# Summing mixture-of-experts rows in memory with weighted accumulating scatters, and fetching expert weights in halves, in a two-layer transformer trunk

## The chip, the cores and the metric

The kernel runs on one core of a Trainium2 chip. The metric is the device time of one execution in microseconds (us). The program is written engine by engine: TensorE (PE), VectorE (DVE), ScalarE (ACT), GpSimd (POOL) and SyncE (SP) each have their own instruction stream, and they meet only at semaphores.

## The reference, cut to what matters

Two layers, each an attention mixer followed by a mixture of experts; 1024 tokens of width 1024, all float32. The change touches the mixture of experts and the norm behind it:

```python
# hier_moe: top-1 group of 4, then top-2 of its 8 experts (32 experts, hidden width 512)
weights = g_gate * jax.nn.softmax(top_val, axis=-1)
h = jax.nn.silu(xb @ w_gate[e]) * (xb @ w_up[e])
out = h @ w_down[e]
y = jax.ops.segment_sum(out * row_w[:, None], row_tok, num_segments=n + 1)[:n]
# behind it, with DEEPNORM_ALPHA = 4 ** 0.25
x = layer_norm(DEEPNORM_ALPHA * x + y, gain, bias)
```

So each token has two (token, expert) pairs, 2048 in all, and the output of a token is the weighted sum of two expert rows.

## The kernel before

Each layer is two blocks of instructions. The first holds the start of the layer (for layer 1 the combine of layer 0: `Combine`) and the attention. The second, written by `Moe.run`, holds the mixer's output product with the first norm and the routing (`MixerOut`), and then the experts.

**Routing.** While TensorE computes the output product tile by tile (8 tiles of 128 tokens), VectorE norms each tile, and for groups of tiles (0 to 2, 3 to 5, 6, 7) it picks the experts (`choose`) and builds one-hot matrices (`select`, lines 1326 and 1327), from which TensorE lists in a PSUM bank which pair stands in which of 128 slots of each expert (`lists`). VectorE writes the list to `slot_rows`, with a column of token numbers and a column of pair numbers (lines 1360 to 1364, `slots_ready`). The two weights of a token (`w_pair`) are computed after that, from two exponentials of ScalarE (`exponentials`, `pair_weights`), token by token and not slot by slot. The normed rows go to `x_rows` in memory (L1078).

**Experts.** Loops over 32 experts, two to an iteration. For each expert POOL gathers its token rows by an indirect DMA (`gather`, L1618, two experts ahead), PE transposes them, and three weight matrices of 2 MB each (gate, up, down) come through one raw buffer each. To keep float32 accuracy each matrix and each input is split into a high and a low part: ScalarE makes the high part (L1769, in halves of 128x2048), VectorE the low one (L346), and PE does three passes (L1547 for gate and up, L1558 for down). SP refills a raw buffer as one DMA once both halves of its low part are made (`refill`, L1481). The result of an expert leaves PSUM by an ACT copy (L1799) and a DVE copy (L1867) into `res[b]`, b being the expert's parity. POOL then scatters it with an indirect DMA to `expert_rows`, one row per pair (`send`, `scatter`, L1624), and waits for it to land before it goes on to the next gather (`ahead`). `res_free` lets ACT and DVE write `res[b]` again once the scatter of two experts ago has landed. After expert 31 the same steps stand for extra blocks of an expert with over 128 rows (`extra_blocks`); none of them runs in the trace.

```python
pool.tensor_copy(row[b], column(e, 1)).then_inc(row_ready, 1)
pool.wait_ge(row_ready, 1 + e + 1)
pool.wait_ge(y_act, 1 + e + 1)
pool.wait_ge(y_dve, 1 + e + 1)
scatter(b, y_out[b])
pool.wait_ge(y_out[b], 16 * (i + 1))
pool.sem_inc(res_free, 1)
```

**Combine.** For each tile SP fetches three arrays of 128x1024: the first and second expert rows and the normed rows (`fetch_rows`, L1906 to L1908), four tiles ahead. The first four tiles are fetched at the end of the experts' block (`first_rows`), in layer 0 with three attention weight fetches behind them (`fetch_job`, L309). A new block starts on the engines once SP too has got to the end of the old one. Per tile ACT scales the first rows into PSUM (L1951), DVE adds the weighted second rows (L1959) and the ALPHA-scaled normed rows (L1963), takes mean and variance (L957 to L960), ACT applies the norm (L977), and POOL multiplies by the gain and adds the bias (L981, L985). In layer 0, PE transposes each tile, ACT and DVE split it, and the first projections of layer 1 start (L627). In layer 1 the tiles go to the output (L1938).

Of the kernel before, what the change touches and what calls it, by code (L numbers as in the profile page):

```python
# [8 lines left out]
F32 = mybir.dt.float32  # L9
# [7 lines left out]
P = 128  # L17
# [20 lines left out]
NO_ROW = 4 * PAIRS  # L38
# [154 lines left out]
def build(nc, x, ab_w_in, ab_w_out, ab_sinks, t5_bias, c_w_in, c_w_out, c_rel_bias, ln_gain, ln_bias,  # L193
          moe_w_group, moe_b_group, moe_w_router, moe_b_router, moe_w_gate, moe_w_up, moe_w_down, out):
    ctx = ExitStack()
    with ctx:
# [6 lines left out]
        o_dram = nc.dram_tensor("expert_rows", [PAIRS, D], F32).ap()  # L203
# [21 lines left out]
        w_pair = sb("w_pair", [P, 2, TILES])  # L225
        slot_rows = sb("slot_rows", [P, BLOCKS, 2], I32)
# [7 lines left out]
        pair_id = sb("pair_id", [P, ENTRIES])  # L234
# [120 lines left out]
        class Load:  # L355
# [3 lines left out]
            def __init__(self):  # L359
# [24 lines left out]
                def gpsimd(pool):  # L384
# [10 lines left out]
                    for group, f0 in zip(ROUTE_GROUPS, ENTRY):  # L395
                        for c in range(2):
                            f, n = f0 + c * len(group), len(group)
                            k.link(pool.iota(pair_id[:, f:f + n], pattern=[[2 * P, n]], base=2 * P * group[0] + c + 1,
                                             channel_multiplier=2, allow_small_or_imprecise_dtypes=True))
# [555 lines left out]
        def norm_begin(dve, rows, t, chain, var_ready):  # L955
# [4 lines left out]
            dve.tensor_scalar(st[:, 14:15], st[:, 13:14], LN_EPS, None, ALU.add).then_inc(var_ready, 1)  # L960
# [13 lines left out]
        def norm_apply(act, rows, t, scale_ready, normed):  # L974
            st = stats[:, t % 4, :]
            act.wait_ge(scale_ready, t + 1)
            act.activation(rows, rows, ACT.Identity, bias=st[:, 17:18], scale=st[:, 16:17]).then_inc(normed, 1)  # L977

        def norm_gain(eng, rows, gain, t, normed, gained):
            eng.wait_ge(normed, t + 1)  # L980
            eng.tensor_tensor(rows, rows, gain, ALU.mult).then_inc(gained, 1)  # L981
# [8 lines left out]
        class MixerOut:  # L990
# [4 lines left out]
            def __init__(self, layer, moe):  # L995
# [7 lines left out]
                 normed, x_turned, x_kept, x1_out, log_ready, log_kept, chain_sem, chosen_sent, rank_ready, ones_sent,  # L1003
                 list_done, slots_ready, exp_sent, exp_done, count_done, extra_sent, extra_done, extras_ready) = sems(
                     *[s + n for s in (
                         "x_in", "par_in", "gain_in", "yh_kept", "yl_kept", "wh_ready", "wl_ready", "mix_ready", "added",
                         "var_ready", "root_ready", "normed", "x_turned", "x_kept", "x1_out", "log_ready",
                         "log_kept", "chain", "chosen_sent", "rank_ready", "ones_sent", "list_done", "slots_ready",
                         "exp_sent", "exp_done", "count_done", "extra_sent", "extra_done", "extras_ready")])
                self.x1_out, self.slots_ready, self.extras_ready = x1_out, slots_ready, extras_ready  # L1010
# [3 lines left out]
                most = 2 * max(len(group) for group in ROUTE_GROUPS)  # L1014

# [1088 lines left out]
```

## Time and profile before

| what | us |
|---|---|
| median of 3 runs | 2539.83 |
| lowest, highest of them | 2538.68, 2542.66 |
| the profiled execution | 2548.89 |
| its span, first to last instruction | 2547.1 |
| PE busy in the span | 2285.8 |
| DVE busy | 1792.9 |
| ACT busy | 1400.6 |
| POOL busy | 514.1 |

The rows further down come from the profiled execution, so times in them are positions in a span of 2547.1 us; layer 0's experts run from about 570 to 1174 us, its combine to about 1262 us, layer 1's experts from about 1877 to 2483 us and its combine to the end. A row of the timeline has the start, the duration, engine, line, operation and operands; in brackets stands how long the engine had been idle before it and what it had waited for. Busy shares of PE are of little use alone; what counts is which wait ends last in each stretch.

### The profile page before, as it was taken

What the parts mean: (1) busy time and instruction counts of PE and PEld (TensorE: products, weight loads), DVE (VectorE), ACT (ScalarE), POOL (GpSimd) and SP (SyncE); (2) the same over time, 40 slices, a digit from 0 to 9 for tenths busy, and PEclk for the clock granted to TensorE, in tenths of its full rate; (3) what the DMA queues carried; (4) which work ended last, traced back from release to release, by engine and by line L of the source; (5) the groups of instructions that cost most, each with busy time, mean ns of one, the idle gap of its engine ahead of it and who ended that gap; (6) DMA issues with size and microseconds to landing.
All of it is one profiled execution on the core that took longest, in us unless ns stands there. A gap on an engine that the chain in (4) does not pass through costs nothing. (4 is left out here: it accounts for less than half of the span.)

```text
span 2547.1 us, 35618 instructions
## 1 busy us (share of the span) xinstructions
PE 2285.8 (90%) x12656; PEld 1860.6 (73%) x12656; DVE 1792.9 (70%) x2475; ACT 1400.6 (55%) x1689; POOL 514.1 (20%) x434
## 2 busy tenths in 40 slices
PE   7999997969999999993699999989969999999980
PEld 6767776857888787882577778867757878887770
DVE  4565546568898889894645555555678988898875
ACT  3454445027877777772344444443057777877743
POOL 0002333012232233321500000000012222332215
PEclk9999998979999999996799999999979999999995
DMA  4110113238999999985411111104069999999956
GB/s 126 24 35 18 34 34 103 91 143 320 371 367 365 371 373 374 369 349 183 169 44 37 44 36 36 36 34 177 34 258 362 381 378 381 378 364 352 361 204 264
DMA packets 127444, 533.53 MB, mean 209 GB/s; under 512 B 36161, under 2 KB 76121, under 8 KB 102761
## 3 DMA queue, kind: packets, MB, share of 16 engines
q1 hardware_dynamic: 108560, 498.44, 52.3%
q0 software_dynamic: 18432, 33.60, 3.5%
q8 instruction: 66, 1.08, 0.2%
q14 instruction: 42, 0.34, 0.0%
q10 hardware_dynamic: 344, 0.08, 0.0%
HBM read 515.21 MB, written 50.39 MB: 222 GB/s over the span
## 5 line engine op out<-in xcount | busy, mean ns | idle before, releaser
L346 DVE TENSOR_TENSOR arena<-arena,arena 128x2048 fp32r<-128x2048 f32 (+1 forms) x458 | 956.5, 2123 | 94.8 <-ACT arena L1769 76.4
L1769 ACT CAST arena<-arena 128x2048 fp32r<-128x2048 f32 x384 | 712.4, 1917 | 140.5 <-PE psum L1547 98.2
L1547 PE MATMUL psum<-arena,arena 128*128 128x512 f32 x3072 | 736.5, 395 | 8.6 <-DVE arena L346 8.6
L1547 PEld LDWEIGHTS psum<-arena,arena 128*128 128x128 f32 x3072 | 570.8, 189 | 124.9 <-issue 6.2
L627 PE MATMUL psum<-arena,arena 128*128 128x512 f32 x2016 | 508.7, 403 | 4.0 <-DVE arena L346 3.1
L627 PEld LDWEIGHTS psum<-arena,arena 128*128 128x128 f32 x2016 | 371.8, 190 | 98.0 <-issue 12.0
L1558 PE MATMUL psum<-arena,arena 128*128 128x512 f32 x1536 | 368.7, 396 | 10.6 <-DVE arena L346 10.6
L1558 PEld LDWEIGHTS psum<-arena,arena 128*128 128x128 f32 x1536 | 288.7, 190 | 85.5 <-DVE arena L346 25.2
L337 PE MATMUL psum<-ident,arena 128*128 128x128 f32 x1024 | 156.9, 295 | 111.9 <-POOL arena L985 39.0
L346 DVE TENSOR_TENSOR arena<-psum,arena 128x512 fp32r<-128x512 f32 (+1 forms) x186 | 161.0, 873 | 130.8 <-ACT arena L1788 64.4
L337 PEld LDWEIGHTS psum<-ident,arena 128*128 128x128 f32 x1024 | 144.8, 197 | 138.9 <-POOL arena L985 42.7
L765 ACT ACTIVATE arena<-arena,arena 128x640 f32<-128x640 f32 (+4 forms) x192 | 120.0, 626 | 193.4 <-DVE arena L847 147.8
L1125 PE MATMUL psum<-arena,arena 128*128 128x512 f32 x768 | 185.3, 397 | 9.3 <-ACT arena L342 6.3
L717 ACT COPY arena<-psum 128x512 f32<-128x512 f32 (+3 forms) x288 | 120.2, 467 | 131.6 <-PE psum L658 131.4
L1615 POOL COPY arena<-slot_rows 128x1 int32 (+1 forms) x64 | 58.1, 907 | 646.8 <-DMA expert_rows<-arena,arena 576.7
L1125 PEld LDWEIGHTS psum<-arena,arena 128*128 128x128 f32 x768 | 142.8, 189 | 39.6 <-issue 6.8
L658 PE MATMUL psum<-ident,arena 128*128 128x128 f32 x888 | 134.5, 283 | 22.2 <-POOL arena L951 9.3
L1618 POOL DMA_INDIRECT arena<-x_rows,arena x64 | 138.0, 2157 | 55.0 <-POOL arena L1615 49.6
L658 PEld LDWEIGHTS psum<-ident,arena 128*128 128x128 f32 x888 | 109.0, 144 | 51.8 <-POOL arena L951 12.1
L680 PE MATMUL psum<-arena,arena 128*64 128x128 f32 x1776 | 131.3, 290 | 0.0
L847 DVE CUSTOM_DVE_ANT_0 arena<-psum,arena 128x640 f32<-128x640 f32 (+3 forms) x192 | 104.9, 572 | 33.6 <-PE psum L646 33.2
L646 PE MATMUL psum<-arena,arena 64*128 64x320 f32 (+5 forms) x1056 | 116.8, 341 | 10.7 <-DVE arena L847 9.5
(155 smaller groups left out, 1783.1 us busy)
## 6 DMA issues: line engine op xcount, KB each, us to landing
arena<-in_moe_w_gate SPq DMA_DIRECT2D x64, 2048.0 KB, 10.8
arena<-in_moe_w_up SPq DMA_DIRECT2D x64, 2048.0 KB
arena<-in_moe_w_down SPq DMA_DIRECT2D x64, 2048.0 KB, 8.9
arena<-expert_rows SPq DMA_DIRECT2D x32, 512.0 KB, 6.7
x_rows<-arena SPq DMA_DIRECT2D x24, 512.0 KB, 2.6
arena<-x_rows SPq DMA_DIRECT2D x24, 512.0 KB, 8.0
arena<-in_c_w_in SPq DMA_DIRECT2D x24, 512.0 KB, 4.1
arena<-in_x SPq DMA_DIRECT2D x16, 512.0 KB, 7.1
```

The source lines that it names most:

```text
L337: m = pe.transpose(dst_bank[:, j * P:(j + 1) * P], rows[:, c0 + j:rows.shape[1]:stride], ident[:])
L346: return eng.tensor_tensor(tile, src, high.bitcast(F32), ALU.subtract)
L627: mm = pe.matmul(job_bank(i, g), w[:, c * P:(c + 1) * P], xs[:, c, half_cols(g)], start=(a == 0), stop=(a == 23))
L658: mm = pe.transpose(bank(B_TURN + h)[:, (b - 4 * g) * P:(b - 4 * g + 1) * P], probs_of(s, h)[:, b * P:(b + 1) * P], ident[:])
L680: mm = pe.matmul(bank(B_OUT)[DH * h:DH * (h + 1), (t % 4) * P:(t % 4 + 1) * P], v_r[pair.kv][:, (kt + b) * P + DH * h:(kt + b) * P + DH * ...
L717: copy(probs_t[s % 2][h][:, a:b], bank(B_TURN + h)[:, 0:b - a]).then_inc(t_copied[h], 1)
L765: act.activation(probs_a[s % 2][h][:, 0:ahead + nk], biased[h][:, 0:ahead + nk], ACT.Exp, bias=low[s % 2][h], scale=-1.0, accum_out=rowsum ...
L1125: return pe.matmul(bank(2 * (t % 2) + half), ys[:, c, t * P:(t + 1) * P], w[:, c, half * BANK:(half + 1) * BANK], start=(k == 0 and c == 0 ...
L1547: mm = pe.matmul(bank(o), cs[:, c * P:(c + 1) * P], ws[:, c * FF:(c + 1) * FF], start=(k == 0 and c == 0), stop=(k == 2 and c == CH - 1))
L1558: mm = pe.matmul(bank(B_Y + s), hs[:, c * P:(c + 1) * P], ws[:, c * D + s * BANK:c * D + (s + 1) * BANK], start=(k == 0 and c == 0), stop= ...
L1618: pool.indirect_dma_start(out=rows[b], out_offset=None, in_=x1_dram, in_offset=bass.IndirectOffsetOnAxis(ap=token[b], axis=0), bounds_chec ...
L1769: act.copy(w_hi[w][:, cols], self.raw[w][:, cols]).then_inc(hi_ready[w], 1)
```

## The change

- `expert_rows` with a row per pair goes; a new array `summed_rows` (`h_dram`) has one row per token. SP writes each normed tile into it, beside the write to `x_rows`. The scatter of each expert adds into it (`compute_op=ALU.add`), at the token's number. Where `slot_rows` had two columns it has one.
- The weights are computed earlier, in three parts for tiles 0 to 2, 3 to 5, and 6 and 7, and are listed slot by slot with the pairs: `lists` multiplies 64 columns instead of 32 for the first two parts, and four more products (`list_weights`) do the last. VectorE keeps them in `slot_weights`.
- For each expert POOL also copies the slot weights to `row_weight[b]`. The two copies out of PSUM become multiplications by it, and wait for it (`weight_ready`).
- A weight fetch of 2 MB becomes two of 1 MB, each with a semaphore of its own: SP refills a half as soon as its low part is made, and ACT starts on a half as soon as it has landed.
- The combine fetches one array per tile. ALPHA goes into the norm's variance and gain; no addition is left. The gain is multiplied by DVE (from PSUM), no longer by POOL. Only two tiles are fetched ahead of the block's end, and the attention weight fetches stand in the next block.

The diff, cut to what this text speaks of (`...` marks what is left out):

```diff
@@MixerOut.sync
                         sp.dma_start(x1_dram[t * P:(t + 1) * P, :], rows_all[:, t, :]).then_inc(x1_out, 16)
+                        sp.dma_start(h_dram[t * P:(t + 1) * P, :], rows_all[:, t, :]).then_inc(h_out, 16)
@@MixerOut.tensor
+                def list_weights(pe):
+                    pe.wait_ge(weights_sent, 1)
+                    for a in range(ENTRIES - late):
+                        mm = pe.matmul(bank(B_LIST)[:, E:2 * E], at_slot[:, a, :], at_block[:, a, E:2 * E],
+                                       start=False, stop=(a == ENTRIES - late - 1), skip_group_check=True)
+                    mm.then_inc(weights_listed, 1)
@@MixerOut.vector
+                def make_weights(dve, L, k):
...
+                    dve.wait_ge(exp_done, k + 1)
+                    L(dve.tensor_reduce(gate[:, ts], gexp[:, ts, :], AX.X, ALU.add))
+                    L(dve.tensor_scalar(near[:, ts], gap[:, ts], 1.0, ALPHA, ALU.add, ALU.mult))
+                    L(dve.tensor_tensor(near[:, ts], near[:, ts], gate[:, ts], ALU.mult))
+                    L(dve.reciprocal(w0, near[:, ts]))
+                    L(dve.tensor_tensor(w1, w0, gap[:, ts], ALU.mult))
...
+                            if g < 2:
+                                dve.tensor_scalar(at_block[:, a, E:2 * E], down_cols[:], key[:, f:f + 1],
+                                                  weight[:, f:f + 1], ALU.is_equal, ALU.mult)
...
                     norm(7)
+                    make_weights(dve, L, 1)
                     select(1)
                     choose(2)
                     keep_logits(7)
                     choose(3)
+                    send_gaps(2)
                     select(2)
                     select(3)
...
-                    L(dve.tensor_copy(slot_rows[:, 0:E, 1], listed))
-                    dve.tensor_scalar(slot_rows[:, 0:E, 0], slot_rows[:, 0:E, 1], 1, None, ALU.arith_shift_right
-                                      ).then_inc(slots_ready, 1)
+                    dve.tensor_copy(slot_rows[:, 0:E], listed).then_inc(slots_ready, 1)
@@Moe.run, SP
-                        sp.wait_ge(lo_ready[w], 1 + 2 * e)
-                        settle(sp)
-                        self.fetch(sp, e, w)
+                        for s in range(2):
+                            sp.wait_ge(lo_ready[w], 1 + 2 * (e - 1) + s + 1)
+                            settle(sp)
+                            self.fetch_half(sp, e, w, s)
@@Moe.run, POOL
-                        pool.indirect_dma_start(out=o_dram, out_offset=bass.IndirectOffsetOnAxis(ap=row[b], axis=0),
+                        pool.indirect_dma_start(out=h_dram, out_offset=bass.IndirectOffsetOnAxis(ap=row[b], axis=0),
                                                 in_=res[b], in_offset=None,
-                                                bounds_check=PAIRS - 1, oob_is_err=False).then_inc(sem, 16)
+                                                bounds_check=SEQ - 1, oob_is_err=False,
+                                                compute_op=ALU.add).then_inc(sem, 16)
...
                     ahead(2, 1, 0)
+                    pool.wait_ge(before.weights_kept, 1)
+                    pool.wait_ge(before.h_out, 16 * TILES)
...
-                        pool.tensor_copy(row[b], column(e, 1)).then_inc(row_ready, 1)
+                        pool.tensor_copy(row_weight[b], column(slot_weights, e)).then_inc(weight_ready, 1)
+                        pool.tensor_copy(row[b], column(slot_rows, e)).then_inc(row_ready, 1)
@@Moe.run, ACT
-                        act.wait_ge(self.raw_in[w], 1 + 16 * (e + 1))
                         act.wait_ge(used[w], 1 + e)
                         for s in range(2):
+                            act.wait_ge(self.raw_in[w][s], 1 + 16 * (e + 1))
...
+                        act.wait_ge(weight_ready, 1 + e + 1)
+                        act.mul(res[b][:, 0:BANK], bank(B_Y), row_weight[b]).then_inc(y_act, 1)
@@Moe.run, DVE
                     split(GATE, 0)
+                    before.send_weights(dve)
                     split(UP, 0)
-                    before.pair_weights(dve)
+                    before.keep_weights(dve)
...
+                        dve.wait_ge(weight_ready, 1 + e + 1)
+                        dve.tensor_scalar(res[b][:, BANK:2 * BANK], bank(B_Y + 1), row_weight[b], None, ALU.mult
+                                          ).then_inc(y_dve, 1)
@@Combine
             def first_rows(self, sp):
-                for t in range(4):
+                for t in range(2):
                     self.fetch_rows(sp, t)
-                if not self.last:
-                    for i in range(3):
-                        fetch_job(sp, 1, i)
...
+                    for t in range(2, TILES):
+                        self.rows_here(sp, t - 2)
+                        self.fetch_rows(sp, t)
+                        if 3 <= t < 6 and not last:
+                            fetch_job(sp, 1, t - 3)
                     for t in range(TILES):
-                        if t + 4 < TILES:
-                            sp.wait_ge(summed, t + 1)
-                            self.fetch_rows(sp, t + 4)
                         sp.wait_ge(shifted, t + 1)
...
                     for t in range(TILES):
-                        norm_gain(pool, rows[t], ln_pars[:, 0, :], t, normed, gained)
                         norm_shift(pool, rows[t], ln_pars[:, 1, :], t, gained, shifted)
...
                     for t in range(TILES):
-                        add(dve, t)
-                        if t >= 1:
-                            norm_scale(dve, t - 1, chain, root_ready, scale_ready)
-                        moments(dve, chain, t)
+                        norm_scale(dve, t, chain, root_ready, scale_ready)
+                        if t + 1 < TILES:
+                            moments(t + 1)
+                        gain(t)
```

How the instructions stand on two engines, before and now. First POOL, one half of an iteration of the experts' loop; DMA on L1618 and L1686 is the gather, on L1624 and L1692 the scatter, `ISA` and `REGISTER_ALU` are register work. Before:

```order
L1615 COPY arena_5574<-slot_rows 128x1
L1616 REGISTER_ALU
L1618 DMA arena_5562<-x_rows,arena_5574 128x1024
L1649 ISA
L1649 COPY arena_5575<-slot_rows 128x1
L1650 REGISTER_ALU
L1624 DMA expert_rows<-arena_5567,arena_5575 2048x1024
```

And now:

```order
L1683 COPY arena_5570<-slot_rows 128x1
L1684 REGISTER_ALU
L1686 DMA arena_5558<-x_rows,arena_5570 128x1024
L1720 ISA
L1720 COPY arena_5573<-slot_weights 128x1
L1721 REGISTER_ALU
L1721 COPY arena_5571<-slot_rows 128x1
L1722 REGISTER_ALU
L1692 DMA summed_rows<-arena_5563,arena_5571 1024x1024
```

One copy, that of the weights, stands between the gather and the copy of the rows; the scatter keeps its place.

Then SP at the end of layer 0's experts, up to the block's end (`UNCONDITIONAL_BRANCH` of L2071, now L2135) and a little beyond; `arena` tiles are on-chip buffers. Before, from the last of the first four tiles:

```order
L1906 DMA arena_5506<-expert_rows 128x1024
L1907 DMA arena_5510<-expert_rows 128x1024
L1908 DMA arena_5514<-x_rows 128x1024
L309 DMA arena_54<-in_c_w_in 128x8x128
L309 DMA arena_55<-in_c_w_in 128x8x128
L309 DMA arena_56<-in_c_w_in 128x8x128
L2071 UNCONDITIONAL_BRANCH
```

And now:

```order
L1984 DMA arena_5506<-summed_rows 128x1024
L1984 DMA arena_5507<-summed_rows 128x1024
L2135 UNCONDITIONAL_BRANCH
L587 UNCONDITIONAL_BRANCH
L1984 DMA arena_5508<-summed_rows 128x1024
L1984 DMA arena_5509<-summed_rows 128x1024
L310 DMA arena_54<-in_c_w_in 128x8x128
```

Fifteen DMAs stood ahead of the block's end; two do now, and the attention weights come behind it.

## Rows read from the trace of the kernel before

**Rows 1.** Stretches: core 0, PE, PEld, DVE, ACT, POOL busy (count), PE clock, DMA, GB/s

```profile
618.20:1132.90 514.70, 505.62 (x2356) 414.73 (x2354) 459.09 (x281) 399.91 (x296) 149.93 (x110) 1.00 0.96 371
1174.40:1262.50 88.10, 29.72 (x137) 24.93 (x137) 51.33 (x86) 32.50 (x46) 40.35 (x16) 0.61 0.62 219
2483.50:2547.10 63.60, 0.00 (x0) 0.00 (x0) 34.73 (x64) 21.16 (x25) 37.38 (x16) 0.50 0.69 264
```

**Rows 2.** Timeline, from layer 0's last scatter to layer 1's first projection

```profile
1169.72 0.98 POOL L1624 DMA_INDIRECT expert_rows<-arena,arena  x1 [12.25 <-DVE arena L1867]
...
1183.09 12.62 SPq L309 DMA_DIRECT2D arena<-in_c_w_in  x3
1196.39 2.15 ACT L1951 ACTIVATE psum<-arena,w_pair 128x1024 f32<-128x1024 f32 x2 [27.73 <-PEq L2071]
...
1240.62 6.68 PE L627 MATMUL psum<-arena,arena 128*128 128x512 f32 x24
```

**Rows 3.** The DMA issues of the page: KB each, median us to landing

```profile
arena<-in_c_w_in SPq DMA_DIRECT2D x24, 512.0 KB, 4.1
```

**Rows 4.** Timeline, DVE in the two combines: layer 0, then layer 1

```profile
1233.56 1.28 DVE L1959 SCALAR_TENSOR_TENSOR psum<-arena,w_pair,psum 128x1024 f32<-128x1024 f32 x1
1234.87 1.22 DVE L1963 SCALAR_TENSOR_TENSOR arena<-arena,psum 128x1024 f32<-128x1024 f32 x1
...
1241.14 1.28 DVE L1959 SCALAR_TENSOR_TENSOR psum<-arena,w_pair,psum 128x1024 f32<-128x1024 f32 x1
...
2503.07 1.28 DVE L1959 SCALAR_TENSOR_TENSOR psum<-arena,w_pair,psum 128x1024 f32<-128x1024 f32 x1
...
2507.47 1.28 DVE L1959 SCALAR_TENSOR_TENSOR psum<-arena,w_pair,psum 128x1024 f32<-128x1024 f32 x1
```

**Rows 5.** The chain that ended last, layer 1's end: start, us, what

```profile
2479.32 3.21 DMA expert_rows<-arena,arena
...
2487.64 10.79 DMA arena<-x_rows
...
2541.69 2.38 POOLq L2071
```

**Rows 6.** Timeline, POOL, one round of the experts' loop in layer 1

```profile
2204.15 1.02 POOL L1624 DMA_INDIRECT expert_rows<-arena,arena  x1 [1.53 <-DVE arena L1867]
2214.37 1.45 POOL L1615 COPY arena<-slot_rows 128x1 int32 x1 [9.20 <-DMA expert_rows<-arena,arena]
2216.67 2.66 POOL L1618 DMA_INDIRECT arena<-x_rows,arena  x1 [0.85 <-POOL arena L1615]
2219.33 1.33 POOL L1649 COPY arena<-slot_rows 128x1 int32 x1
2222.20 1.02 POOL L1624 DMA_INDIRECT expert_rows<-arena,arena  x1 [1.53 <-DVE arena L1867]
```

**Rows 7.** Waits of POOL, 600 to 1140 us: total, times, longest

```profile
POOL arena L1615 <- DMA expert_rows<-arena,arena: 289.2, 28, 13.1
```

**Rows 8.** Timeline, POOL, after a scatter late in layer 0's experts

```profile
1138.26 0.18 POOL L1649 COPY arena<-slot_rows 128x1 int32<-128x1 int32 x1 [2.41 <-DMA expert_rows<-arena,arena]
```

**Rows 9.** The DMA queues of the page: packets, MB, share of 16 engines

```profile
q1 hardware_dynamic: 108560, 498.44, 52.3%
q0 software_dynamic: 18432, 33.60, 3.5%
```

**Rows 10.** Timeline, DVE in layer 0's routing and at the experts' start

```profile
504.95 0.20 DVE L1248 TENSOR_TENSOR logits<-psum,b_route 128x36 f32<-128x36 f32 x1 [2.52 <-PE psum L1097]
...
545.19 0.28 DVE L1326 TENSOR_SCALAR arena<-iota_cols,arena 128x128 f32<-128x128 f32 x1
545.39 0.30 DVE L1327 TENSOR_SCALAR arena<-down_cols,arena,pair_id 128x32 f32<-128x32 f32 x1
...
567.60 0.18 DVE L1375 TENSOR_REDUCE arena<-arena 128x8 f32<-128x32 f32 x1
...
568.96 1.22 DVE L346 TENSOR_TENSOR arena<-psum,arena 128x1024 fp32r<-128x1024 f32 x1
```

**Rows 11.** The chain that ended last, layer 1's second expert: start, us, what

```profile
1939.93 11.43 DMA arena<-in_moe_w_up
```

More of the change, by code:

```diff
@@ L952, in _, with norm_begin @@
                                                left[h][:, SEQ - nk:SEQ], ALU.subtract).then_inc(p_ready[h], 1)
-        def norm_begin(dve, rows, t, chain, var_ready):
+        def norm_begin(dve, rows, t, chain, var_ready, factor=1.0):
             st = stats[:, t % 4, :]
@@ L972, in norm_scale, with norm_apply, norm_gain @@
                               ).then_inc(scale_ready, 1)
-        def norm_apply(act, rows, t, scale_ready, normed):
+        def norm_apply(act, out, rows, t, scale_ready, normed):
             st = stats[:, t % 4, :]
             act.wait_ge(scale_ready, t + 1)
[L977 to L981, printed above, removed]
+            act.activation(out, rows, ACT.Identity, bias=st[:, 17:18], scale=st[:, 16:17]).then_inc(normed, 1)
+        def norm_gain(dve, rows, src, factor, gain, t, normed, gained):
+            dve.wait_ge(normed, t + 1)
+            dve.scalar_tensor_tensor(out=rows, in0=src, scalar=factor, in1=gain, op0=ALU.mult, op1=ALU.mult
+                                     ).then_inc(gained, 1)
         def norm_shift(pool, rows, shift, t, gained, shifted):
@@ L1032, in __init__ @@
                 rank = place(AT_CHOICE + 1, ENTRIES)
+                weight = place(AT_CHOICE + 1.0625, ENTRIES)
                 count_row = place(AT_CHOICE + 1.25, E)
@@ L1309, in choose, with send_gaps @@
                             L(ins)
+                    def send_gaps(k):
+                        ts = WEIGHT_TILES[k]
+                        nt = ts.stop - ts.start
+                        L(dve.tensor_tensor(gexp[:, ts, :], logits[:, ts, 0:G],
+                                            gmax[:, ts].unsqueeze(2).to_broadcast([P, nt, G]), ALU.subtract))
+                        dve.tensor_tensor(gap[:, ts], m2[:, ts], m1[:, ts], ALU.subtract).then_inc(exp_sent, 1)
                     def select(g):
@@ L1511, in run @@
                 row = [pen(8)[:, 0:1].bitcast(I32) for _ in range(2)]
+                row_weight = [pen(8)[:, 0:1] for _ in range(2)]
                 assert pen.kb <= AT_GATE - 12
@@ L1703, in _ @@
                     pe.wait_ge(rows_ready, 1 + 1)
+                    before.list_weights(pe)
                     turn(0, 0, 0)
@@ L1772, in _ @@
                     split(GATE, 0)
+                    before.exponentials(act, 2)
                     split(UP, 0)
-                    before.exponentials(act)
                     act.wait_ge(before.x1_out, 16 * TILES)
+                    act.wait_ge(before.h_out, 16 * TILES)
                     act.wait_ge(xt_ready, 1 + 1)
```

200 lines of the change are left out of this document (106 added, 94 removed).

## The prediction

> **What bounds the kernel now.** I first cut the span into stretches. In the experts' loop [rows 1] TensorE is busy 505.6 of 514.7 us at its full clock of 2.4 GHz, and the DMA engines are busy 0.96 of the time: two resources near their limit together. 28 experts take 514.7 us, 18.38 us each. The two combines are another matter. Layer 0's takes 88.1 us with PE busy for 29.7 of them at a mean clock of 0.61; layer 1's takes 63.6 us with no PE work at all. Neither is bound by work: DVE, the busiest, has 51.3 and 34.7 us.
>
> Then the timeline across layer 0's combine [rows 2]. The last scatter is issued at 1169.72. ACT starts its first scaling at 1196.39, 26.7 us later, released at the block's end, which SP reached only when it had got rid of three weight fetches that took it 12.62 us from 1183.09 on. The twelve row fetches ahead of them fill the queue. In layer 1 the chain that ended last [rows 5] goes from the last scatter (landed at 2482.5) through row fetches (a piece of 10.79 us) and then down POOL's gain and bias to the end.
>
> **The change, term by term**, on the profiled execution's span of 2547.1 us.
>
> *Layer 0's combine.* SP now has two fetches before the block's end. I let the last scatter land 1 us later than now (below), which puts the first fetch at 1175.4; a fetch of 512 KB lands after about 4.1 us [rows 3], on empty queues 3.5 (I choose the lower), so DVE begins near 1179. Its work per tile falls from 7.58 us (1233.56 to 1241.14 [rows 4]) by the two additions of 1.28 and 1.22, and rises by one multiplication out of PSUM like L1959, 1.28: 6.36 us where splits of tiles and weights lie between, and 4.40 - 1.22 = 3.18 without them. Moments and first root take 2.5 us; tiles 0 to 2 at 3.2, tile 3 at 4.6, tiles 4 and 5 at 6.4, and a part of tile 6 until tile 3's low part is made (4.6) give 1179 + 2.5 + 9.6 + 4.6 + 12.8 + 4.6 = 1213. There PE starts the first projection, now at 1240.62 [rows 2]: 27 us earlier. From there to the stretch's end at 1262.5 it is PE and its transposes as before. I take **-26**.
>
> *Layer 1's combine.* First fetch at 2484.5, rows at 2488, scale at 2490.5, seven tiles at 3.2, a last one at 3.1, the bias on POOL 2.4 and the store 3.1 (the end now comes 5.4 us after 2541.69 [rows 5], of which POOL has 2.38): 2521.5. I take **-25**; POOL, with one pass per tile in place of two, is no longer the pace; DVE's 3.2 is, and ACT's one pass per tile fits beside it.
>
> *Routing.* From tile 7's norm to the list DVE is late and has next to no idle time. A small operation costs 0.20 there (545.19 to 545.39 [rows 10]); chained ones 0.22 (six between 567.60 and 568.96). Added ahead of `slots_ready`: five chained for the weights of part 1 (1.1), six one-hots (1.2), `send_gaps` (0.4); one conversion goes (-0.2): +2.5. Behind it: weights of part 2 and four one-hots (1.9) and a copy (0.2), against the 1.36 of `pair_weights` and the 0.4 of the old exponent inputs: +0.3, and I add 0.5 for PE's four products in front of the first transposes. **+3.3 per layer, +6.6**. The same additions for part 0 lie in a gap of 2.52 in which DVE waits for the router's logits [rows 10], against 2.2 added, and cost nothing; if that cover went, it would be 2.2. The table changes of ACT for its early exponentials lie in its long waits for DVE's variances. The eight more writes of rows are issued while the queue has little else; only tile 7's stands in front of the first up weights (about 1.3 us at the rate of the page), and half fetches give that back.
>
> *The experts' loop, ACT and DVE.* One pass out of PSUM stays one pass. Two more semaphore waits lie on the ACT path that delays the second expert of an iteration; at 0.05 to 0.1 each, **+4** over 32 iterations (ends: 0 and 8). In layer 1 ACT twice waited for up weights, once with a landing of 11.43 [rows 11], at about 1 us lost each; a half arrives sooner: **-1.6**.
>
> *The experts' loop, POOL.* This is the place that can go wrong. Before, nobody but POOL waited for the ring scatter, landing, gather, copy; ACT and DVE only needed a scatter two experts back. Now both stop in front of `weight_ready`, and behind them stand the next SiLU and both next splits. The ring [rows 6]: scatter 1.02, landing 9.20, token copy 1.45, 0.85, gather 2.66, copy 1.33, and then only 1.53 us, most of it handover, until the next scatter: 18.05 in all. With the weight copy in the row copy's place, evacuations (0.7, an estimate: half of the 1.28 of a pass twice as wide [rows 4]) and handover (1.0 of the 1.53) behind it, the new ring is 9.0 plus the landing, or 8.6 with a shorter token copy; it sets the pace once landings exceed about 9.6. They now average 289.2 / 28 = 10.3 in the stretch [rows 7], so they must become shorter. Uncontended, the landing takes 2.41 [rows 8]: some 7 us are the weight traffic. One 2 MB fetch occupies the engines for 52.3% x 2547.1 x 2.10 / 498.44 = 5.6 us [rows 9], so this is a little over one fetch. With fetches of half the size I expect the 7 us to become about 4. The accumulation is in no row. Below, it costs nothing more than the plain scatter; above, each row is read and written, one after the other, as if the scatter came twice, 2.41 us. I take 1.3, since only the reading is new (the software queue's 3.5% is 0.7 us a transfer, on half the engines if valid rows stand in the first slots 1.4). Landing: 2.4 + 4 + 1.3 = 7.7, two below the limit. **0**.
>
> The Trainium skill, page "DMA: Bandwidth & Descriptors", section "Queues, rings and completion order", says that each DMA engine goes round its queues and changes only at the end of a packet of several descriptors. By that the scatter waits for at most the packet in progress, which a half fetch halves, and the term would be the same 0; the landings agree that the waiting is about one fetch. The skill's page "Collectives: The Full Stack", section "Part 3: Why 7× under link rate — side-by-side accounting", speaks against the change: an addition in a DMA needs two reads per piece, so it delivers half as fast. No row here shows an accumulation; by that rule the landing would still be under the limit.
>
> Sum: 2547.1 - 26 - 25 + 6.6 + 4 - 1.6 = 2505, which is 42 less. The profiled execution took 2548.89, 9 us over the median of 2539.83, so the median becomes **2498**.
>
> **Rivals.**
>
> *A, POOL sets the pace (slower).* If halves don't shorten the landing and the addition costs 1.4, it is 11.7 and the ring 20.3: 1.9 us over 18.4, for 62 experts 118 us, 2616. It decides from 0.65 us per expert on (40 / 62), a landing of about 10.3. For it: the landings of 13.1 and a ring that is already full. Against: 2.41 alone, which says the length is that of the traffic. 14%.
>
> *B, the DMA engines become the bound.* Per expert, three fetches of 5.6 and two indirect transfers of 0.7 make 18.2 of 18.38 us [rows 9]; a further 0.7 for the reading makes 18.9, 0.5 too much for 62 experts: 31 us, 2529. For it: the 0.96 [rows 1]. Against: packets stretched by each other are in these shares, and halves refill earlier. 12%.
>
> *C, the combines are paced by fetches.* Only two are in flight; at 8 us to landing instead of 4 that is 4 us a tile and not 3.2, and with exchanges between DVE and ACT no better than now each gains some 8 us less: 2514. 12%.
>
> *D, it is a wash*: several of these partly, 2535 to 2545. 2%.
>
> **How the numbers follow.** The forecast has 60%. A measurement of this kernel can tell 0.2%, 5 us, from no change. All of the forecast, B and C and none of A lie below 2534.8: faster 0.84, same 0.02, slower 0.14. The range leaves out A: it starts 14 us under the forecast (loop terms at their low ends, combines 5 us better each) and goes up to 2535, over B.
>
> **What would show it.** The span from the last scatter of layer 0 to the first projection falls from 71 to 44 us; ACT or DVE starts the combine within 8 us of the scatter's landing; the last 63.6 us become about 38. DVE sets 3.2 us per tile in layer 1. The experts' period stays 18.3 to 18.5 us, the median landing of the scatter is 6 to 9 us, and POOL waits for DVE before it scatters. Wrong it would be if the evacuations waited for POOL's weight copy and PE showed idle time before gate or down products at a period over 18.7; B would show as ACT waiting for weights.

## The result and the profile after

The changed kernel takes **2559.74 us** (median of 5 runs, 2554.12 to 2569.66) against 2539.83 of before (2538.68 to 2554.17, 5 runs): a ratio of 1.0068 with a 95% interval of 1.0043 to 1.0092, slower by 0.7%. The prediction was 2498, faster by 1.6%. The profiled execution took 2569.66 us, with a span of 2567.9 against 2547.1 before: 20.8 more.

I cut both spans at five places that a timeline names: the first gate product (PE's first product with an expert's gate weights) and the last scatter of each layer, and the end. The last column has the terms of my sum.

| stretch | before | after | difference | my terms |
|---|---|---|---|---|
| start to first gate product, layer 0 | 570.33 | 589.10 | +18.8 | +3.3 |
| experts, layer 0, to the last scatter | 599.4 | 618.5 | +19.1 | +2 |
| last scatter to first gate product, layer 1 | 706.9 | 699.2 | -7.7 | -26 + 3.3 |
| experts, layer 1, to the last scatter | 602.7 | 616.0 | +13.3 | +0.4 |
| last scatter to the end | 67.8 | 45.1 | -22.7 | -25 |

**The combines** did what the change says. Layer 0's last scatter, SP's first fetches, DVE's first moments and PE's first projection, in the timeline after (columns: start us, us, engine, line, operation, tiles, idle time before and its releaser), where [rows 2] stood:

```profile
1207.58 1.57 POOL L1692 DMA_INDIRECT summed_rows<-arena,arena  x1 [12.07 <-issue]
...
1214.85 6.36 SPq L1984 DMA_DIRECT2D arena<-summed_rows  x4
...
1220.55 0.69 DVE L959 BATCH_NORM_STATS2 stats<-arena 128x6 f32<-128x512 f32 x1 [10.69 <-PEq L2135]
...
1224.49 1.21 DVE L983 SCALAR_TENSOR_TENSOR arena<-psum,arena 128x1024 f32<-128x1024 f32 x1
...
1227.56 1.22 DVE L983 SCALAR_TENSOR_TENSOR arena<-psum,arena 128x1024 f32<-128x1024 f32 x1
...
1254.73 6.99 PE L628 MATMUL psum<-arena,arena 128*128 128x512 f32 x24
```

From scatter to projection it is 47.2 us, before 70.9. DVE begins 13 us after the scatter; before, the first instruction, ACT's, came 26.7 us after it. Without splits DVE makes a tile in 3.07 us (1224.49 to 1227.56). Layer 1's combine does the same, 22.7 us less.

**The experts' loop** got slower. A pair of experts (one iteration) takes 38.06 us in the median, before 36.76. The waits between 700 and 1150 us, of the kernel before and then of the change (us in total, times, longest):

```profile
POOL arena L1615 <- DMA expert_rows<-arena,arena: 240.7, 23, 13.1
...
PE psum L337 <- DVE arena L1852: 5.3, 12, 0.4
```

```profile
POOL arena L1683 <- DMA summed_rows<-arena,arena: 196.6, 24, 9.0
...
ACT arena L1876 <- POOL arena L1720: 31.6, 11, 2.9
...
PE psum L338 <- DVE arena L1931: 19.8, 12, 1.8
```

The landing (the time until a scatter's rows are in memory) did become shorter. But ACT's evacuation (L1876) waited for POOL's weight copy (L1720) in 11 of the 24 experts there, once per iteration, and PE waits at the transposes of the hidden rows (L338) for DVE's product of gate and up (L1931) 12 times, once per iteration, 1.2 us longer each (19.8 less 5.3, by 12). The timeline of one iteration shows why it is every second expert; PE's two down products are L1625:

```profile
943.88 1.61 POOL L1692 DMA_INDIRECT summed_rows<-arena,arena  x1 [1.83 <-DVE arena L1947]
...
952.53 0.75 PE L338 MATMUL psum<-ident,arena 128*128 128x128 f32 x4 [1.74 <-DVE arena L1931]
...
955.33 5.74 PE L1625 MATMUL psum<-arena,arena 128*128 128x512 f32 x24 [0.20 <-DVE arena L347]
...
958.41 1.31 POOL L1720 COPY arena<-slot_weights 128x1 f32 x1
...
961.11 0.69 ACT L1876 ACTIVATE arena<-psum,arena 128x512 f32<-128x512 f32 x1 [2.15 <-PE psum L1625]
...
963.52 1.61 POOL L1692 DMA_INDIRECT summed_rows<-arena,arena  x1 [1.59 <-DVE arena L1947]
...
972.96 2.21 POOL L1683 COPY arena<-slot_rows 128x1 int32 x1 [7.83 <-DMA summed_rows<-arena,arena]
...
973.22 5.62 PE L1625 MATMUL psum<-arena,arena 128*128 128x512 f32 x24
...
976.02 2.64 POOL L1686 DMA_INDIRECT arena<-x_rows,arena  x1 [0.85 <-POOL arena L1683]
...
978.66 1.31 POOL L1720 COPY arena<-slot_weights 128x1 f32 x1
...
980.09 0.69 ACT L1876 ACTIVATE arena<-psum,arena 128x512 f32<-128x512 f32 x1 [2.87 <-POOL arena L1720]
```

The two experts of an iteration are not alike. From a scatter to the end of the next down product it is 943.88 to 961.07, 17.2 us, on one side and 963.52 to 978.84, 15.3 us, on the other. POOL's scatter, landing, token copy, gather and weight copy take 15.8 and 16.5 us. On the first side the weight is 1.4 us early; on the second it is 1.1 us late, and both evacuations with it. Behind ACT's stand the next SiLU, the copies of the next tokens and two splits, and behind these DVE's product, for which PE then waits 1.74 us (0.4 before).

**The experts' start** takes longer in both layers, in three pieces. The first is in the mixer's product. ACT's instructions from the norm's root of tile 3 to that of tile 4, before and then after:

```profile
482.58 0.20 ACT L965 ACTIVATE stats<-stats 128x1 f32<-128x1 f32 x1 [9.30 <-DVE stats L960]
486.38 1.02 ACT L1198 COPY arena<-psum 128x1024 f32<-128x1024 f32 x1 [3.60 <-PE psum L337]
496.68 0.20 ACT L965 ACTIVATE stats<-stats 128x1 f32<-128x1 f32 x1 [9.28 <-DVE stats L960]
```

```profile
485.85 0.20 ACT L967 ACTIVATE stats<-stats 128x1 f32<-128x1 f32 x1 [9.28 <-DVE stats L962]
486.07 1.28 ACT L1240 ACT_TABLE_LOAD   x1
494.42 0.21 ACT L1240 ACTIVATE arena<-arena 128x12 f32<-128x12 f32 x1 [7.07 <-DVE arena L1361]
...
494.64 0.99 ACT L1220 COPY arena<-psum 128x1024 f32<-128x1024 f32 x1
...
506.73 0.20 ACT L967 ACTIVATE stats<-stats 128x1 f32<-128x1 f32 x1 [9.80 <-DVE stats L962]
```

The copy of the turned rows (L1198, now L1220) used to come 3.8 us after the root. Now the early exponentials stand ahead of it, and wait until DVE has finished choosing the experts of the first three tiles (part 0). The copy comes 8.8 us after the root, PE waits for it with the router's product, and the next root comes 20.9 us after the last instead of 14.1: **+6.8**. The other two pieces lie behind it. From tile 7's root to POOL's first token copy it is 21.1 instead of 18.8 us, **+2.3**. From that copy to the first transposes it is 13.5 instead of 7.0, **+6.5**:

```profile
558.72 0.20 POOL L1615 COPY arena<-slot_rows 128x1 int32<-128x1 int32 x1 [19.93 <-DVE slot_rows L1364]
558.79 8.89 DVE L346 TENSOR_TENSOR arena<-arena,arena 128x2048 fp32r<-128x2048 f32 x4
...
559.92 2.27 POOL L1618 DMA_INDIRECT arena<-x_rows,arena  x1 [0.99 <-POOL arena L1615]
...
563.31 0.33 SPq L1481 DMA_DIRECT2D arena<-in_moe_w_gate  x1
...
565.68 1.95 PE L337 MATMUL psum<-ident,arena 128*128 128x128 f32 x8 [8.06 <-DMA arena<-x_rows,arena]
```

```profile
570.85 4.49 DVE L347 TENSOR_TENSOR arena<-arena,arena 128x2048 fp32r<-128x2048 f32 x2
571.07 2.12 POOL L1683 COPY arena<-slot_rows 128x1 int32<-128x1 int32 x1 [22.22 <-DVE slot_rows L1424]
574.19 2.26 POOL L1686 DMA_INDIRECT arena<-x_rows,arena  x1 [1.00 <-POOL arena L1683]
...
575.37 0.80 SPq L1543 DMA_DIRECT2D arena<-in_moe_w_gate  x2
...
584.60 1.97 PE L338 MATMUL psum<-ident,arena 128*128 128x128 f32 x8 [5.40 <-DMA arena<-x_rows,arena]
```

Before, two small operations of DVE (the old inputs of the exponentials) stood between the list and the first weight split, and POOL's copy slipped in ahead of the split by 0.07 us. Now the split follows the list at once, and the copy takes as long as the split's first half. The gather leaves when SP is already issuing the gate fetch that the same split released, and lands 10.4 us after its issue began, not 5.8.

So per layer 15.6 us at the start, 32.4 us in both loops, -23.8 and -22.7 us in the combines: +17.1. Most of the remaining 3.7 us lie in layer 0 ahead of all that: the first norm root already comes 1.7 us later, and the roots of tiles 1 and 2 are 11.4 us apart and not 9.8, with a granted clock of 0.93 in 450 to 500 us where it was 1.00 (in e4, which leaves this part as it was, they are 11.4 apart too). In the profiles of this study the first root lies between 444.7 and 452.7 us, which is why I judge every experiment by its stretches and not by its median alone.

### The profile page after: what moved, and what is told of

It is laid out like the page before. It is cut to its first block and busy times, and to the rows that moved or that the text cites. A ratio compares the mean times of both kernels' runs of the same rounds, so it can differ in the third digit from the quotient of the medians.

```text
span 2567.9 us, 36470 instructions
## 1 busy us (share of the span) xinstructions
PE 2305.8 (90%) x12672; PEld 1877.3 (73%) x12672; DVE 1788.5 (70%) x2519; ACT 1400.7 (55%) x1689; POOL 646.6 (25%) x482
## 5 line engine op out<-in xcount | busy, mean ns | idle before, releaser
L628 PEld LDWEIGHTS psum<-arena,arena 128*128 128x128 f32 x2016 | 372.9, 191 | 97.7 <-issue 11.6
L1625 PE MATMUL psum<-arena,arena 128*128 128x512 f32 x1536 | 369.7, 397 | 8.6 <-DVE arena L347 8.6
L1625 PEld LDWEIGHTS psum<-arena,arena 128*128 128x128 f32 x1536 | 290.9, 191 | 82.1 <-DVE arena L347 20.9
L338 PE MATMUL psum<-ident,arena 128*128 128x128 f32 x1024 | 157.5, 296 | 112.9 <-DVE arena L1931 50.4
L338 PEld LDWEIGHTS psum<-ident,arena 128*128 128x128 f32 x1024 | 145.5, 198 | 140.3 <-DVE arena L1931 64.4
L1683 POOL COPY arena<-slot_rows 128x1 int32 (+1 forms) x64 | 69.9, 1092 | 532.9 <-DMA summed_rows<-arena,arena 459.9
L1686 POOL DMA_INDIRECT arena<-x_rows,arena x64 | 174.7, 2729 | 55.0 <-POOL arena L1683 55.0
L1692 POOL DMA_INDIRECT summed_rows<-arena,arena x64 | 102.9, 1607 | 187.5 <-DVE arena L1947 175.5
L1876 ACT ACTIVATE arena<-psum,arena 128x512 f32<-128x512 f32 x64 | 44.0, 688 | 173.5 <-PE psum L1625 106.9
```

Of the source, the lines that this page charges most:

```text
L338: m = pe.transpose(dst_bank[:, j * P:(j + 1) * P], rows[:, c0 + j:rows.shape[1]:stride], ident[:])
L628: mm = pe.matmul(job_bank(i, g), w[:, c * P:(c + 1) * P], xs[:, c, half_cols(g)], start=(a == 0), stop=(a == 23))
L1625: mm = pe.matmul(bank(B_Y + s), hs[:, c * P:(c + 1) * P], ws[:, c * D + s * BANK:c * D + (s + 1) * BANK], start=(k == 0 and c == 0), stop= ...
L1686: pool.indirect_dma_start(out=rows[b], out_offset=None, in_=x1_dram, in_offset=bass.IndirectOffsetOnAxis(ap=token[b], axis=0), bounds_chec ...
```

## Experiments

**My theory** was then: three separate losses, (a) the weight copy at the end of POOL's ring, (b) the early exponentials in front of a copy, (c) the token copy beside the split. The rivals: the DMA engines set the pace because of the addition (rival B), the halves cost more than they bring, or the second set of row writes delays the start.

| run | median us | ratio to before (95%) | experts, layers 0, 1 | median pair | last scatter to end |
|---|---|---|---|---|---|
| change | 2559.74 | 1.0068 (1.0043 to 1.0092) | 618.5, 616.0 | 38.06 | 45.1 |
| e1 weights early | 2534.26 | 0.9952 (0.9935 to 0.9969) | 602.2, 602.0 | 36.84 | 45.3 |
| e2 plain scatter | 2522.78 | 0.9912 (0.9889 to 0.9936) | 600.2, 601.3 | 36.84 | 42.1 |
| e3 whole fetches | 2598.91 | 1.0211 (1.0178 to 1.0244) | 639.9, 635.7 | 39.66 | 45.1 |
| e4 before, halves | 2543.27 | 1.0000 (0.9984 to 1.0017) | 600.4, 600.1 | 36.75 | 68.2 |
| e5 exponentials later | 2551.68 | 1.0033 (1.0017 to 1.0049) | 616.5, 617.1 | 38.06 | 45.5 |
| e6 weights before split | 2549.87 | 1.0022 (1.0008 to 1.0036) | 616.0, 617.6 | 38.05 | 45.5 |
| e7 e1 + e5 + e6 | 2506.09 | 0.9867 (0.9838 to 0.9895) | 602.7, 601.6 | 36.87 | 45.4 |
| e8 tokens early | 2529.53 | 0.9953 (0.9939 to 0.9968) | 602.2, 602.0 | 36.87 | 45.6 |
| e9 weight last | 2585.77 | 1.0156 (1.0128 to 1.0183) | 626.5, 626.3 | 38.58 | 45.4 |
| e10 all early | 2502.82 | 0.9845 (0.9829 to 0.9861) | 602.2, 601.6 | 36.86 | 45.3 |

**e1: the weight copy ahead of the landing.**

```diff
+                    def weigh(e, b):
+                        pool.tensor_copy(row_weight[b], column(slot_weights, e)).then_inc(weight_ready, 1)
+
+                    weigh(0, 0)
+
                     def send(e, i, b):
...
-                        pool.tensor_copy(row_weight[b], column(slot_weights, e)).then_inc(weight_ready, 1)
                         pool.tensor_copy(row[b], column(slot_rows, e)).then_inc(row_ready, 1)
...
                         scatter(b, y_out[b])
+                        if not isinstance(e, int) or e < EXPERTS - 1:
+                            weigh(e + 1, 1 - b)
...
                         pool.wait_ge(y_out[b], 16 * (i + 1))
```

> The changed kernel, with GpSimd copying the next expert's weight column right behind its scatter and no longer behind the landing, token copy and gather. Theory (the weight copy at the end of GpSimd's ring delays the evacuations of every second expert by about 1.2 us, and TensorE's hidden transposes with them): ACT and DVE no longer wait for the weight copy, a pair of experts takes 36.7 to 37.0 us instead of 38.06, the time falls by 30 to 38 us, to 2522 to 2530. Rival (the DMA engines set the pace, because of the addition's reads or the halves): waits move to the weights, a pair stays above 37.6 us, and the time stays at 2550 to 2560.

The pair is at 36.84 and 30 us of the loops are gone (16.3 and 14.0). The median fell by 25.5, less than the 30 to 38 that I had given, and lies above my 2522 to 2530. By the ratios it is 29 us: the kernel before, measured again beside each group of runs, had medians from 2539.8 to 2542.3. No evacuation waits for POOL. The scatter lands no sooner than in the change (10.1 us from issue, there 9.5), and the DMA engines are busier than there (0.98 of the time against 0.96), so neither of these was the bound. But their waits did appear, as rival B said (waits of e1, 700 to 1150 us), and they cost a little that the median pair does not show: both loops take 1204.2 us here and 1201.5 in e2.

```profile
ACT arena L1850 <- DMA arena<-in_moe_w_gate: 28.0, 22, 2.3
...
PE psum L338 <- DVE arena L1937: 6.8, 12, 0.6
```

**e2: a scatter that overwrites** (`compute_op=ALU.add` taken away; the sums are left out).

> The changed kernel with a scatter that overwrites in place of one that adds (the sums over a token's two experts and its own row are left out). Theory: the addition costs 0.6 us at the issue and about 2 us of landing, so the landing falls from 9.4 to 7 to 8 us from the issue, the weight copy comes early enough, and the loop runs at about 36.9 us a pair; each combine begins 2.5 us earlier. Together 35 to 42 us less, 2518 to 2526. Rival (the landing is all weight traffic, the addition costs nothing beyond its issue): pairs at 37.5 to 38 us, 2545 to 2560. Rival (reads of the addition load the DMA engines): also a fall, but with DMA's share visibly lower and waits for weights gone.

The landing falls from 9.5 to 7.7 us, the pair to 36.84, the last stretch by 3.0 us. The addition thus costs 1.8 us from issue to landing in the loop, 0.6 of it at the issue itself, and 3.0 us at the end. The DMA issues of 700 to 1150 us (median us to landing), of the change, of this run and of e4:

```profile
summed_rows<-arena,arena POOLq DMA_INDIRECT x23, 9.5
```

```profile
summed_rows<-arena,arena POOLq DMA_INDIRECT x25, 7.7
```

```profile
expert_rows<-arena,arena POOLq DMA_INDIRECT x24, 7.8
```

**e3: whole fetches in the change** (one transfer of 2 MB a matrix, released by the second low part, as before).

> The changed kernel with each weight matrix fetched by one transfer of 2 MB again. Theory: the scatter lands 1.5 to 3 us later, GpSimd's ring of 9.0 us plus the landing then exceeds 18.4 us for every expert, and the loop takes 20 to 21 us an expert: 2600 to 2680. Rival (two issues and two semaphores a matrix cost more than they bring): the time falls, to 2540 or lower.

A hair under its low end: 39 us over the change, 19.8 an expert and not 20 to 21. ACT now waits for the weight copy (here L1719) in 22 of 23 experts:

```profile
ACT arena L1876 <- POOL arena L1719: 77.6, 22, 5.0
```

From copy to first transposes it is still 13.1 us: the halves are not what delays the start.

**e4: halves in the kernel before.**

> The kernel before with weight fetches in halves, nothing else. Theory (halves only shorten what waits in the queues, and nothing there waits for them but the few up weights of layer 1): within 5 us of the kernel before, 2533 to 2542, the scatter's landing 1 to 3 us shorter than the 10.3 us wait of before. Rival (halves burden SyncE and the DMA engines): slower than before by 10 to 30 us.

No change in time: the ratio is 1.0000, and the median lies 1 us above the 2533 to 2542 that I had given. The landing falls by 3.6 us, from 11.4 to 7.8. POOL alone waits for it, and nobody waits for POOL. From copy to first transposes it is 7.0 and 6.9 us.

**e5: the exponentials behind the copy.**

```diff
-                        if t == 7:
-                            exponentials(act, 1)
+                        if t in (4, 7):
+                            exponentials(act, t // 7)
                         norm_root(act, t, var_ready, root_ready)
-                        if t == 3:
-                            exponentials(act, 0)
```

> The changed kernel with ACT's exponentials of the first three tiles behind its copy of tile 3's turned rows, no longer ahead of it. Theory (ACT stands in front of the exponentials until DVE has finished the whole choice of part 0, and the router's product of tile 3 and every later tile wait behind it): the interval between the norm roots of tiles 3 and 4 falls from 20.9 to 14.1 us in both layers, 13 us less, 2544 to 2550. Rival (the 6.8 us are the two table loads or the added writes of rows): the interval stays over 19 us and the time at 2555 to 2562.

The roots of tiles 3 and 4 stand 14.1 us apart again in both layers, and the table load behind the copy is still there, in a wait of 9 us:

```profile
477.43 0.20 ACT L967 ACTIVATE stats<-stats 128x1 f32<-128x1 f32 x1 [9.28 <-DVE stats L962]
481.24 1.02 ACT L1220 COPY arena<-psum 128x1024 f32<-128x1024 f32 x1 [3.60 <-PE psum L338]
482.27 1.28 ACT L1238 ACT_TABLE_LOAD   x1
...
491.54 0.20 ACT L967 ACTIVATE stats<-stats 128x1 f32<-128x1 f32 x1 [3.90 <-DVE stats L962]
```

The median fell by 8.1 us where the two intervals give 13.6; it lies 2 us above what I expected. The interval of its ratio touches the change's, so it is the stretch that shows this gain and not the median.

**e6: the last weights ahead of the first split** (`before.send_weights(dve)` moved up in front of `split(GATE, 0)`).

> The changed kernel with DVE making the last tiles' weights and one-hots ahead of the first weight split, no longer behind it. Theory (GpSimd's copy of the token column took 2.12 us beside the split instead of 0.2, the gather then left together with the gate fetch that the split releases, and landed 5 us later): from the copy to the first transposes 7 to 8 us instead of 13.5, in both layers; 10 to 13 us less, 2547 to 2551. Rival (the gather is slow because of the weight halves or the second set of row writes in the queues): 12 to 13.5 us as now, no gain.

From copy to first transposes it is now 5.5 us in both layers, 8 us less. But the next token copy met the splits:

```profile
570.13 0.19 POOL L1683 COPY arena<-slot_rows 128x1 int32<-128x1 int32 x1 [22.24 <-DVE slot_rows L1424]
...
571.32 1.24 POOL L1686 DMA_INDIRECT arena<-x_rows,arena  x1 [1.00 <-POOL arena L1683]
571.79 8.88 DVE L347 TENSOR_TENSOR arena<-arena,arena 128x2048 fp32r<-128x2048 f32 x4
...
572.58 8.14 POOL L1683 COPY arena<-slot_rows 128x1 int32<-128x1 int32 x1
...
575.66 1.97 PE L338 MATMUL psum<-ident,arena 128*128 128x128 f32 x8 [1.76 <-DMA arena<-x_rows,arena]
...
582.05 1.19 PE L1614 MATMUL psum<-arena,arena 128*128 128x512 f32 x2 [4.42 <-DVE arena L347]
```

DVE's low part of the first rows now comes behind four splits, so the first gate product follows the copy by 11.9 us (18.0 in the change, 11.6 before): 6.1 us gained there. The median fell by 9.9, the low end of what I had given.

**e7: all three.**

> The changed kernel with all three: weight columns copied ahead of the landing, exponentials behind the copy, last weights ahead of the split. Theory: the three losses are separate stretches and add up, 25 + 13 + 12 us under the changed kernel: 2505 to 2514. Rival (they overlap, or one delay hides behind another): 2518 to 2530.

2506.09: 53.6 us under the change and 1.3% under the kernel before. By the ratios to before, the three singly took away 1.2%, 0.4% and 0.5% (of 0.7% slower), together 2.0%; e7 took away 2.0%. The losses add up, and the rival of overlapping losses is out.

**e8: only the token copy ahead of the landing**, the weight copy left where it was (the column for expert e + 4 is copied behind scatter e; the gather stays).

> The changed kernel with only the token column of the gather after next copied ahead of the landing; the weight copy stays behind landing and gather. Theory (what counts is when GpSimd's weight copy ends against the end of the down product, whichever piece of the ring is taken out): the weight comes 1.4 to 3 us earlier, no evacuation waits for it, a pair takes 36.8 to 36.9 us, 2530 to 2540. Rival (the evacuations suffer from the weight copy itself standing beside them, not from its being late): a pair stays at 38 us, 2555 to 2560.

36.87 us a pair, and 2529.53, half a microsecond under the range that I had given. It is not the weight copy as such that costs; it is when it ends.

**e9: the two copies in the other order**, rows first, weight second.

> The changed kernel with GpSimd's two copies in the other order, the scatter's rows first and the weights second. Theory: the row copy takes 0.2 us on one side of a pair and up to 2.2 on the other, where DVE is in a split, and both now stand ahead of the evacuations: a pair takes 38.3 to 40 us, 2565 to 2620. Rival (no dependence on the copy's time): 2555 to 2562.

38.58 us a pair, and 8 and 10 us more than the change in the two loops. Both sides are late now (waits of e9, 700 to 1150 us):

```profile
ACT arena L1876 <- POOL arena L1721: 71.4, 23, 3.2
```

**e10: the three, and every copy of POOL ahead of the landing**, both first token columns ahead of the first gather.

> The three fixes, and in addition token and row columns copied ahead of the landing, and at the start of the experts both token columns copied ahead of the first gather (the second one took 8.14 us beside the splits with the three fixes). Theory: the loop is at TensorE's pace already, so only the start gains, 0 to 4 us a layer: 2499 to 2506. Rival (something of GpSimd's ring still shows in the loop): a pair falls under 36.7 us and the time under 2498.

2502.82, the fastest, 1.5% under the kernel before; the interval overlaps with e7's, so the two can't be told apart. The pair does not fall: POOL no longer sets anything in the loop. At the start the second gather's own issue takes 8.65 us beside the splits in place of the copy, and nothing is gained there.

## Why the prediction was wrong

**The ring, "it sets the pace once landings exceed about 9.6": this is the step that failed.** I held POOL's ring against the mean period of 18.4 us, but the weight copy must be in time on each side of a pair. From a scatter to the end of the next down product it is 15.4 us on one side and 16.2 on the other already in the kernel before (medians from 700 to 1150 us), 15.3 and 16.3 in e1 and e2. By my own terms [rows 6] scatter, token copy, handover, gather and weight copy take 1.02 + 1.45 + 0.85 + 2.66 + 1.33 = 7.3 us beside the landing, which leaves 8.0 on the short side. I had the landing at 7.7, "two below the limit"; it was 0.3 below.

Three parts then came out larger, in the round above: the issue of the adding scatter 1.61 us and not 1.02, the token copy 2.21 beside a split and not 1.45, POOL's wait for the landing 7.83 (8.2 in the mean, 196.6 / 24). So the weight copy ends 16.45 us after the scatter began, where my terms give 15.0, and 1.1 us after the down product of the short side, once a pair. The whole ring is 18.4 us there (963.52 to 981.93), 10.6 of it beside the landing and not 9.0.

That is rival A in its mechanism and not in its size: I gave it 14% and priced it at 118 us, because I took 20.3 us for every expert; the loops lost 32.4. Its sign, evacuations that wait for POOL's weight copy at a period over 18.7, is what the trace shows: the period is 19.03. e1, e8 and e9 show the cause from three sides: the copy moved away, another piece taken out, 0.2 to 2.2 us put in.

**The addition, 1.3 us: right for the wait, and the issue was in no term.** Under load POOL waits 8.2 us for a landing in the mean, and 7.1 in e2 (168.7 and 8.8 us in 25 waits): 1.1 more. The issue takes 1.6 us instead of 1.02. With little else in the queues the addition costs what I had as the upper end: POOL waits 4.74 us for a landing late in layer 0, where it was 2.41 [rows 8] (timeline of the change):

```profile
1178.14 2.25 POOL L1720 COPY arena<-slot_weights 128x1 f32<-128x1 f32 x1 [4.74 <-DMA summed_rows<-arena,arena]
```

The software queue (packets, MB, share of 16 engines) in the 10 us from layer 0's last scatter, with no gather under way, before (1169.7 to 1179.7) and after (1207.5 to 1217.5):

```profile
q0 software_dynamic: 144, 0.37, 9.3%
```

```profile
q0 software_dynamic: 144, 0.37, 25.8%
```

The same packets take 2.8 times as long. From 700 to 1150 us the queue has 7.4% in e2 and 10.6% in the change, but half of its transfers are gathers. If these still cost what they do in e2, 0.69 us each, a scatter went from 0.69 to 1.35 us, about twice (an estimate from these two shares); the 0.7 us more is what I gave rival B. The Trainium skill's "Collectives: The Full Stack", section "Part 3: Why 7× under link rate — side-by-side accounting", says half the rate because of two reads; the estimate under load agrees, and with little else in the queues it was more than that.

**Halves.** I expected some 3 us less landing and no other cost. e4 gives -3.6, and e3 that the change would be 39 us slower without them.

**Routing, +3.3 a layer: the operations ahead of the list, +2.5, measured +2.3.** What failed is the sentence that ACT's table changes "lie in its long waits for DVE's variances". I looked at what the exponentials themselves take and not at what stands behind them: the copy of the turned rows. e5 shows +6.8 a layer, and that the table loads really are free.

**The start, +0.3 and +0.5 behind the list: it was +6.5.** I cost the removed exponent inputs of DVE as 0.4 us gained. They were what kept POOL's copy ahead of the split. e6 shows it, and e3 and e4 show that the halves have no part in it.

**Combines, -26 and -25: right in mechanism, over 2 us too large each** (-23.8 and -22.7). I let the last scatter land 1 us later; e2 shows 3.0 for the addition in the last stretch. DVE's pace was 3.07 where I had 3.2, so fetches don't set it, and rival C is out.

**The small terms of the loop, +4 and -1.6.** Both loops take 1202.1 us before, 1200.5 in e4, 1201.5 in e2 and 1204.2 in e1. The halves give -1.6 in sum, but as +1.0 in layer 0 and -2.6 in layer 1, which is not how I had it. With the ring out of the way the rest is +3.7 in e1 (e7, e8 and e10 are within half a microsecond of it), of which 2.7 comes only with the adding scatter. So the sum of the two fits, and partly by luck.

**Rival B** is half right: with the ring out of the way the DMA engines are at 0.98 and ACT waits for gate weights 22 times in 24 experts, but the cost is those 2.7 us and not 31.

With the losses away the time comes near the forecast: e7 and e10, which keep the change's combines, scatter and halves, take 2506 and 2503 us where I had forecast 2498 for the change itself. That supports the terms for combines and loops together. It doesn't save the forecast, which was for a kernel without these repairs.

## What to carry to other kernels

A new wait is judged at the shortest interval in which it must be met, not at the mean period: list both sides of an unrolled loop, with the time from the release to the need, and price each piece as it runs beside the others. Here the room was 0.3 us where the mean showed two, and a longer issue and a slower copy used it up. What a producer can prepare ahead of its own long wait (here three columns of 512 B) should stand ahead of it. And when an operation is inserted or removed, ask what stands behind it in its engine's order and which small operations kept another engine's slot open, not only how long it takes itself.

## What the runs showed of the hardware

A copy of one column on POOL takes 0.2 us, and 2.12 us when a DVE operation with two on-chip inputs began 0.2 us earlier (571.07 to 573.19, the end of the split's first half). The Trainium skill's "SBUF — State Buffer", section "🔬 SBUF: two separate sides", says that a GpSimd operation that reads on-chip memory and a VectorE operation with two such inputs share a port pair by an exclusive lock that is held for a whole instruction, and that agrees with the 2.12. The 8.14 of e6 is more than one instruction: there the copy waited out four splits in a row, 572.58 to 580.72, the last of which ended at 580.67. Elsewhere (972.96) the next gap was enough. What decides this isn't settled by these runs.

Four runs give the scatter's landing under load for both kinds and both sizes of fetch: plain 11.4 with 2 MB fetches and 7.8 with 1 MB, adding 11.3 (in a loop that runs 8% slower, with the engines at 0.93) and 9.5. The weights' queue moved 14.3 KB per packet before and 7.2 in e4 (152.40 MB in 10678 packets, 152.16 in 21048), at the same 366 to 367 GB/s in all. Whether the landing became shorter by the smaller packets or by less weight traffic issued at a time, no run here separates.
